# A chunked delta-rule scan: two alternating places for the memory, the query's read moved behind the output product

## What is computed

```python
def step(state, inp):
    w_c, u_c, attn_c, q_c, k_c, e_c = inp
    v_new = u_c - einsum('bhcd,bhde->bhce', w_c, state)
    o_c = einsum('bhcd,bhde->bhce', q_c, state) + einsum('bhcm,bhme->bhce', attn_c, v_new)
    state = state * e_c[..., None, None] + einsum('bhcd,bhce->bhde', k_c, v_new)
    return state, o_c
s0 = zeros((bsz, nh, dk, dv))
_, o = lax.scan(step, s0, ...)
```

## Time and profile before

| | |
|---|---|
| runs, median (range) | 2157.25 us (2155.11 to 2157.98) |
| the profiled execution: span from first to last instruction | 2150.7 us |
| what lies around that span, by the runs | 4.4 to 7.3 us; the profiled execution's own whole time isn't on the page |
| instructions | 20753 |
| PE busy | 2070.0 us |
| DVE busy | 1364.1 us |
| ACT busy | 642.5 us |
| POOL busy | 234.5 us |
| mean granted clock of PE | 0.993 |
| DMA | 207.17 MB, mean 96 GB/s |

### The profile page before, as it was taken

How to read it: one execution, slowest core, us unless ns; L and a number is a source line. 1 busy time by engine, 2 the same in 40 slices (tenths; PEclk the granted TensorE clock), 3 DMA queues, 4 the chain that set the end, 5 groups by cost and what they waited for, 6 DMA issues and landing times. The chain is left out here.

```text
span 2150.7 us, 20753 instructions
## 1 busy us (share of the span) xinstructions
PE 2070.0 (96%) x6898; PEld 1060.6 (49%) x6898; DVE 1364.1 (63%) x1918; ACT 642.5 (30%) x1063; POOL 234.5 (11%) x188
## 2 busy tenths in 40 slices
PE   6999999999999999999899899999999999999998
PEld 5444444446555556566555445554444444444443
DVE  4687753265746746647652578529999997534633
ACT  4345431323443434434311521012321111241021
POOL 0000001112212113122100400001000000003200
PEclk8999999999999999999999999999999999999999
DMA  9333389241111111111420316269722222334021
GB/s 342 110 109 100 116 272 236 89 92 35 47 29 37 38 37 37 24 36 43 147 41 1 108 59 120 74 189 250 173 59 75 68 73 69 103 103 137 20 98 59
DMA packets 243824, 207.17 MB, mean 96 GB/s; under 512 B 52204, under 2 KB 202785, under 8 KB 243745
## 3 DMA queue, kind: packets, MB, share of 16 engines
q1 hardware_dynamic: 213393, 157.25, 24.5%
q0 software_dynamic: 13056, 42.99, 8.2%
q10 hardware_dynamic: 17312, 6.10, 1.2%
HBM read 182.55 MB, written 60.33 MB: 113 GB/s over the span
## 5 line engine op out<-in xcount | busy, mean ns | idle before, releaser
L2300 PE MATMUL bank<-hT,ring 128*128 128x512 f32 x576 | 254.2, 592 | 0.0
L2300 PE MATMUL bank<-resid,ring 128*128 128x512 f32 x432 | 191.3, 592 | 0.0
L2300 PEld LDWEIGHTS bank<-hT,ring 128*128 128x128 f32 x576 | 109.5, 190 | 137.7 <-issue 136.7
L1279 PE MATMUL bank<-hT,ring 128*128 128x512 f32 x336 | 157.7, 595 | 1.8 <-ACT silu_z L1515 1.8
L3220 DVE SCALAR_TENSOR_TENSOR yT<-s_arena,yT 128x1024 f32<-128x1024 f32 x120 | 153.8, 1282 | 0.0
L3220 DVE SCALAR_TENSOR_TENSOR s_arena<-s_arena 128x1024 f32<-128x1024 f32 x112 | 143.5, 1282 | 0.0
L2272 PE MATMUL bank<-hT,ring 128*128 128x512 f32 x320 | 139.4, 594 | 0.0
L2300 PEld LDWEIGHTS bank<-resid,ring 128*128 128x128 f32 x432 | 82.1, 190 | 103.3 <-issue 102.3
L1869 DVE SCALAR_TENSOR_TENSOR memory<-memory,col_exp_last,bank 128x128 f32<-128x128 f32 x64 | 22.3, 348 | 153.7 <-PE bank L1459 153.7
L2272 PEld LDWEIGHTS bank<-hT,ring 128*128 128x128 f32 x320 | 60.2, 190 | 73.7 <-issue 73.4
L2345 PE MATMUL bank<-ssm_y,ring 128*128 128x512 f32 x192 | 83.4, 592 | 0.0
(11 more groups left out here) (585 smaller groups left out, 3671.7 us busy)
## 6 DMA issues: line engine op xcount, KB each, us to landing
ada<-in_ada_w SPq DMA_DIRECT2D x8, 2048.0 KB, 8.1
ring<-in_gdn_in_w SPq DMA_DIRECT2D x32, 512.0 KB, 4.1
ring<-in_w_in SPq DMA_DIRECT2D x54, 256.0 KB, 2.9
ab_U_sums<-in_w_in POOLq DMA_DIRECT2D x6, 2048.0 KB, 19.0
resid<-in_x SPq DMA_DIRECT2D x8, 1024.0 KB, 8.9
ring<-in_lru_in_w SPq DMA_DIRECT2D x16, 512.0 KB, 3.9
ring<-ab_U_sums SPq DMA_DIRECT2D x32, 256.0 KB, 3.0
lru_arena<-in_ada_w SPq DMA_DIRECT2D x6, 1024.0 KB, 12.5
```

The costliest lines, as they stand in the source:

```text
L1279: last = nc.tensor.matmul(bank[:, to, :], w[:, k, :], v[:, k, :], start=(first and k == 0), stop=(k == KB - 1), skip_group_check=not only)
L2300: last = nc.tensor.matmul(bank[:, to, :], w[:, k, :], src[:, k, :], start=(start and k == 0), stop=(k == HK - 1), skip_group_check=not alone)
```

## The change

The memory gets two places that alternate: chunk c reads place c % 2 and its update writes place (c + 1) % 2. The query's read of chunks 1 to 6 moves behind the chunk's output product and gets a mark (`q`); in chunk 7 it stands between the first fill and "new". Chunk 0 has neither read nor query's read nor delta nor output sum: "new" takes the values directly, and DVE copies the memory product into place 1. Chunk 7 has no memory product and no update. The wait for ACT's output step moves from the query's read to "new"; the update gets a wait for the update before it, the output sum one for the query's read. Chunk 0 has one fill fewer in middle heads, and the fills ahead of `k_flip` become 5; in head 7 the counts stay the same in sum (0 and 4 in place of 2 and 2 in chunk 0). The memset goes.

```diff
-            memory = sb("memory", [P, P], scope)
+            memory = sb("memory", [P, 2, P], scope)
...
+            def scan_products(c):
+
+                if c == 0:
+                    return ("new", "mem", "o")
+                return ("read", "new", "mem", "o", "q") if c < NCH - 1 else ("read", "q", "new", "o")
+
+            def scan_sums(c):
+
+                return ("mem",) if c == 0 else ("delta", "mem", "o") if c < NCH - 1 else ("delta", "o")
...
-                        fill(4, 0)
+                        fill(5, 0)
...
-                        for c in range(NCH):
-                            if c == 0:
-                                fill(1, 0)
-                                hd_dve.wait(pe, "invT64b", h)
-                                hd_dve.wait(pe, "mem_zero", h)
-                                hd_dve.wait(pe, "v_tok", h)
-                            else:
-                                hd_dve.wait(pe, f"mem{c - 1}", h)
-                            hd_pe.mark(nc.tensor.matmul(R4[:, 0, :], kT[:, c, :], memory[:, :], start=True, stop=True), f"read{c}")
-                            if c:
+                        def read(c):
+
+                            hd_dve.wait(pe, f"mem{c - 1}", h)
+                            hd_pe.mark(nc.tensor.matmul(R4[:, 0, :], kT[:, c, :], memory[:, c % 2, :], start=True, stop=True), f"read{c}")
+
+                        def query_read(c):
+
+                            if c > 1:
                                 hd_dve.wait(pe, f"o{c - 1}", h)
-                                hd_act.wait(pe, f"o{c - 1}", h)
-
-                            nc.tensor.matmul(R5[:, 4, :], qT[:, c, :], memory[:, :], start=True, stop=True)
+                            hd_pe.mark(nc.tensor.matmul(R5[:, 4, :], qT[:, c, :], memory[:, c % 2, :], start=True, stop=True), f"q{c}")
+
+                        def solve(c, right):
+
+                            hd_pe.mark(nc.tensor.matmul(R4[:, 4, :], invT[:, c, :], right, start=True, stop=True), f"new{c}")
+
+                        def use(c):
+
+                            hd_act.wait(pe, f"new{c}", h)
+                            if c < NCH - 1:
+                                hd_dve.wait(pe, "k_rest", h)
+                                hd_pe.mark(nc.tensor.matmul(R5[:, 0, :], k_rest[:, c, :], delta[:, 1, :], start=True, stop=True), f"mem{c}")
+                            hd_pe.mark(nc.tensor.matmul(R4[:, 4, :], attnT[:, c, :], delta[:, 1, :], start=True, stop=True), f"o{c}")
+
+                        fill(1, 0)
+                        hd_dve.wait(pe, "invT64b", h)
+                        hd_dve.wait(pe, "v_tok", h)
+                        solve(0, v_tok[:, 0, :])
+                        fill(1, 4)
+                        use(0)
+                        for c in range(1, NCH):
+                            read(c)
                             fill(1, 2)
+                            if c == NCH - 1:
+                                query_read(c)
                             hd_dve.wait(pe, f"delta{c}", h)
-                            hd_pe.mark(nc.tensor.matmul(R4[:, 4, :], invT[:, c, :], delta[:, 0, :], start=True, stop=True), f"new{c}")
+                            hd_act.wait(pe, f"o{c - 1}", h)
+                            solve(c, delta[:, 0, :])
                             fill(1, 2)
...
+                            use(c)
+                            if c < NCH - 1:
+                                query_read(c)
...
-                        hd_dve.wait(act, f"o{c}", h)
+                        if c:
+                            hd_dve.wait(act, f"o{c}", h)
+                        else:
+                            hd_act.wait(act, "o0", h)
...
-                        hd_pe.wait(dve, f"o{NCH - 1}", h, back=1)
-                        hd_dve.mark(dve.memset(memory[:, :], 0.0), "mem_zero")
-                        for c in range(NCH):
+                        hd_pe.wait(dve, "mem0", h)
+                        hd_dve.mark(dve.tensor_copy(memory[:, 1, :], R5[:, 0, :]), "mem0")
+                        for c in range(1, NCH):
...
-                            hd_pe.wait(dve, f"mem{c}", h)
-                            hd_dve.mark(dve.scalar_tensor_tensor(out=memory[:, :], in0=memory[:, :], scalar=cols["exp_last"][:, h, c:c + 1],
-                                                                 in1=R5[:, 0, :], op0=ALU.mult, op1=ALU.add), f"mem{c}")
+                            if c < NCH - 1:
+                                hd_pe.wait(dve, f"mem{c}", h)
+                                hd_dve.wait(dve, f"mem{c - 1}", h)
+                                hd_dve.mark(dve.scalar_tensor_tensor(out=memory[:, (c + 1) % 2, :], in0=memory[:, c % 2, :],
+                                                                     scalar=cols["exp_last"][:, h, c:c + 1],
+                                                                     in1=R5[:, 0, :], op0=ALU.mult, op1=ALU.add), f"mem{c}")
                             hd_act.wait(dve, f"o{c}", h)
+                            hd_pe.wait(dve, f"q{c}", h)
```

More of the change, by code:

```diff
@@ L1023, in block_program @@
             o_tok, o_normed = part0[:, :, :], AT
-            memory = sb("memory", [P, P], scope)
+            memory = sb("memory", [P, 2, P], scope)
             delta = sb("delta", [P, 2, P], scope)
             g_rows = delta[0:HEADS * NCH, 0, :]
-            fold_ab = memory[:, 0:2 * HEADS]
+            fold_ab = memory[:, 0, 0:2 * HEADS]
             g_dram = nc.dram_tensor("g_scratch", (HEADS * NCH, P), F32, kind="Internal").ap()
@@ L1038, in halves @@
                 return [n + x for n in names for x in "ab"]
+            def scan_products(c):
[4 more added lines that the diff above has]
+                return ("mem",) if c == 0 else ("delta", "mem", "o") if c < NCH - 1 else ("delta", "o")
             hd_pe = Steps(sem("gdn_pe"), ["k_flip", "kk", "q_flip", "qk"]
                           + [n for s in levels for n in halves(f"Y{s}") + (["v_flip"] if s == levels[0] else []) + halves(f"YT{s}") + (halves(f"F{s}") if s < 64 else [])]
-                          + [f"{n}{c}" for c in range(NCH) for n in ("read", "new", "mem", "o")] + ["o_flip"])
+                          + [f"{n}{c}" for c in range(NCH) for n in scan_products(c)] + ["o_flip"])
             hd_act = Steps(sem("gdn_act"), ["k_sq", "decay", "q_silu", "q_sq", "k_rms", "v_silu"]
@@ L1053, in block_program @@
                            + [n for s in levels for n in halves(f"invT{s}") + (["q_inv", "q_dec"] if s == levels[1] else [])]
-                           + ["mem_zero"] + [f"{n}{c}" for c in range(NCH) for n in ("delta", "mem", "o")]
+                           + [f"{n}{c}" for c in range(NCH) for n in scan_sums(c)]
                            + ["o_inv", "o_tok", "y"])
```

## The result

The changed kernel takes 2119.49 us (median of 4 runs, 2117.52 to 2120.40), against 2157.48 us (4 runs) of the kernel before on the same chip: ratio 0.983, 95% interval 0.9815 to 0.9846, 38.0 us less. The forecast was 2115.8. The profiled execution took 2120.4 us, its span 2118.5.

A forecast was written before the change was run, and what follows sets the result against it. PE, 96% busy, idles 0.97 us per 3.79 us chunk, mostly at the query's read waiting for DVE's output sum. Seven middle scans 35.5 plus last head 6.0 make 41.5 us: 2157.25 - 41.5 = 2115.8 us, range 2109 to 2127.

The forecast's parts named there:

- Steady chunks: Chunks 1 to 6 of a middle scan: 3.30 us from read to read in place of 3.79, 0.49 less each.
- First and last chunk: Middle scan: first chunk 1.52 us shorter, with the copy taken as 0.29; last chunk 0.61 shorter.
- The moved fill: Fifth fill ahead of the key flip, seven times: fits PE's hole to 0.1 us; cost 0, bound 6.0 us.
- Last head: Last head's scan: 1.26 us less in the first chunk, 0.68 in six, 0.69 in the last; 6.0 in sum.
- From the barrier on: Next stage behind the last head: a barrier opens it and its loads are issued relative to it; no change priced.
- The span: Profiled span of the whole kernel: 2150.7 less 41.5, so 2109.2 us.
- 1 (met waits free, 3.18): Added met waits cost nothing: 0.61 us less per steady chunk, 46.5 in sum, time 2110.8; chance 0.20.
- 2 (gain handed back at the seams): Moved fill costs 6.0 us, or query's read doesn't fit behind output product, 9.2: 2121.8 or 2125.0; chance 0.12.
- 3 (copy locked out by POOL): First chunk's new DVE copy held by POOL sums, up to 1.27 us in seven heads, 8.9: 2124.7; chance 0.04.
- Rival 4 (lockstep): Output sum waits for the query's read and delays the next delta: all 48 chunks pay 0.3, 2171.6; chance 0.02.
- 5: Another chain (ring loads, clock) holds the head, scan's gain becomes a wait: 2157, chance 0.02; half lost, 2136, 0.04.
- the rule quoted in the prediction: At the new copy: copies and tensor-scalars can enter a two-port mode locking out GpSimd and themselves for the whole instruction.

The follow-up runs named there:

- d: Kernel before with two memory places and the moved query's read, ends and fills as before, no update wait for the update before it: 2126.36 us, 0.9862.
- g: Changed kernel with a third, always-met wait at the update, behind the other two: 2122.78 us, 0.9845.
- h: Changed kernel with the moved fill put back into chunk 0 (four ahead of the key flip, two behind the first "new"): 2122.97 us, 0.9844.
- a: Changed kernel measured again without edit: 2120.66 us, 0.9832.
- j: Changed kernel measured a third time without edit: 2119.61 us, 0.9833 against the kernel before at 2155.76.
- b: Kernel before, unedited, a single execution again: 2157.16 us, span 2155.2.
- f: Changed kernel with the met waits written ahead of the one that counts, at the update, "new" and the output sum: 2112.41 us, 0.9791.
- k: Changed kernel with met waits ahead of the counting ones and the update's wait for the update before it left out: 2111.94 us, 0.9794.
- c: Kernel before with two alternating memory places alone, nothing moved: 2155.52 us, 0.9995.
- e: Changed kernel with the query's read put back between read and fill in chunks 1 to 7: 2143.67 us, 0.9949.

## Why the prediction was right, and what it missed

The sign, the mechanism and the parts held; the median came out 3.7 us above the forecast, inside the range (2109 to 2127). Against the kernel before on the same chip the gain was 38.0, 36.4 and 36.2 us, 3.5 to 5.3 short of the 41.5. Step by step:

- *Steady chunks.* Forecast 3.30 us, measured 3.30. Right, also in the split: 0.61 from the moved read (d has 3.22), 0.08 given back at the update (d against the changed kernel) and 0.03 to 0.05 at "new". The price, 0.08 for a met wait behind the one that counts, came from one row of another engine, and g doubled it on DVE. In the last head the same query's read, with the same two waits, loads 0.06 behind the sum (1146.37 + 0.35 to the 1146.78 of the earlier trace rows), so no price is paid there; the last section has why.
- *First and last chunk.* The copy measured 0.29, as taken between its bounds, and the read stands at 517.32 (forecast 517.38); from the last read to the last output product it is 2.49, as worked out. Scan 24.42, forecast 24.4.
- *The moved fill.* Forecast: the flip slips by up to 0.1, priced at 0. It slips 0.09 at each flip of heads 1 to 6. With the scan's 5.02 in place of 5.07 this is the missing 1.0 us of 41.5: 7 x 0.14. h shows the other side: without the move each head is 0.86 longer. In head 0 the slip is taken up too, but not where the prediction had it: the key flip is 0.92 later, the query flip, whose wait of 0.46 us is gone, 0.30 later, and the value flip comes at 499.66 for 499.73, with a wait of 0.72 for 0.80 (0.83 and 0.82 in a and j).
- *Last head.* Forecast 6.0 less, measured 6.06; reads 4.81 apart. The start of its scan was to move from 1140.25 to 1104.8 and is at 1105.77.
- *From the barrier on.* This is the step that failed: "behind the last head a barrier opens the next stage, whose loads are issued relative to it", so the next block's time was taken as unchanged. It is 1.9 us longer, by the granted clock of its first 47 us. 1.0 and 1.9 make 2.9 of the 3.7 us. The rest isn't placed. In the traces the first "new" of head 0 stands anywhere from 512.5 to 519.2 us, with no order by version, and the three pairs of medians differ among themselves by 1.8 us.
- *The span.* 2109.2 was forecast and 2118.5 measured, 9.3 more: 1.0 and 1.9 as above, and 6.4 at the loads of yT, since the profile of before was of an execution in which they came early (6.2 of it came back in b). The same kernel again had a span of 2155.2. The prediction saw that the runs lay above that profile by 4.4 to 7.3 us and used the median for the time. What lies around the span is 1.9 or 2.0 us in every run since, so that execution took some 2152.6 us, less than any of the three runs beside it; it could have asked which stretch of the profile was the short one.

The rivals: 1 (met waits free, 3.18) was wrong for the kernel as changed and is right for the same waits in another order (f). 2 (gain handed back at the seams) is refuted by the flip at 548.48 without idle time, by 0.44 from memory product to query's read, and by h. 3 (copy locked out by POOL): all eight copies take 291 or 292 ns, and six of them run wholly within a POOL sum, such as the copy of head 0 (516.97 to 517.26):

```profile
L1888 DVE COPY memory<-bank x8: 291/291/292, 517.0 to 1110.0; 128x128 f32<-128x128 f32 x8
516.55 1.27 POOL L1227 TENSOR_TENSOR yT<-ring 128x512 f32<-128x512 f32 x1 [10.43 <-DMA ring<-in_gdn_in_w]
```

None of the six is stretched (in h no POOL operation falls on a copy, and they take 291 to 293 ns), so this POOL operation doesn't lock the copy out. The Trainium skill, VectorE: DVE Perf Modes, Mode 2×_2P, says that mode doesn't exist for an operand in PSUM, as DVE has one read port there. The trace agrees; it is the reading that the rule quoted in the prediction lacked. Rival 4 (lockstep): delta still waits for PE by 0.17, so the sum is never late. 5: the scan's gain arrives at the barrier, but for the 0.09 us at each seam.

## What to carry to other kernels

Price each link of a loop that PE and another engine hand back and forth, one by one, and look for work that stands in such a link although its result is wanted only later; here one 0.22 us product cost 0.61. In a loop whose index is in a register, write waits that are long met ahead of the wait that decides: here the order alone was worth 5.5 to 6 us of 2120 by the traces (the medians fell by 7 to 8). In straight-line code with constants the decisive one belongs first. And compare a stretch that a change shouldn't touch with a second profile of the same kernel before a difference there is explained.

## What was not expected of the hardware

- Order of waits. In the heads whose index is in a loop register a met wait costs 0.08 to 0.09 us behind the deciding one (memory product to update 0.52, 0.60, 0.69 us with none, one, two of them) and nothing ahead of it (f and k both 3.18). The traces show what fills the time: register operations of 40 ns on the queue, about 0.09 apart. One at the update's own line stands ahead of each update of the middle heads, in every version; in the changed kernel these are 42 of the 48.

```profile
L1902 DVEq ALU_OP  x42: 40/40/40, 520.1 to 1011.7; - x42
```

  For each further wait that is written behind the deciding one, one more stands at the line of `wait` (L58). In g there are two, ahead of the update of 520.80:

```profile
L58 DVEq ALU_OP  x2: 40/40/40, 520.5 to 520.6; - x2
```

  The handover goes by their number: 0.42 us with none (the copy in all heads, and the updates of the last head where no separate wait stands ahead of them, as below), 0.51 to 0.52 with one (d, f, k), 0.60 with two, 0.69 with three. In k the one that is left starts 0.09 ahead of the update that waited, so it stands behind the wait and not under it. A kernel that works these values out ahead of the wait wasn't tried.
- In the last head, whose numbers are constants, there are no register operations and the order is reversed: met wait ahead 0.49 to 0.50 us from memory product to update (1126.79 to 1127.29 in f), behind it or absent 0.42 (1114.34 to 1114.76 in the changed kernel). PE's query's read reverses too: behind the end of the output sum it loads after 0.12 us in the middle heads and 0.05 in the last with the met wait behind (c), and after 0.05 and 0.12 with it ahead (e). The trace of f has a separate wait instruction right ahead of that update:

```profile
L58 DVEq EVENT_SEMAPHORE  x1: 21/21/21, 1127.2 to 1127.2; - x1
```

  It starts 0.43 behind the memory product, about when a lone wait's update starts, and the update follows 0.07 later. By the semaphores in the trace it waits for PE, that is, it is the wait that was written last. In the changed kernel the separate one is again the wait written last, there the long met one: it stands ahead of the memory product and costs nothing. The Trainium skill, Perfetto Trace Analysis, Identifying Dependency Chains, says that an instruction which waits on several engines may get separate wait instructions ahead of it. The trace agrees for the last head (21 ns each here); which wait becomes the separate one the page doesn't say.
- The granted clock behind a barrier: the same instructions, with the last 20 us ahead at the full clock, fall to 1.2 GHz once, twice or three times within 32 us, according to the version (first part 45.6 to 47.5 us), and the two versions that were traced more than once repeat their own pattern (g, whose scans are 0.09 a chunk longer, shares that of the changed kernel). What sets it stays open.
- The wait for scattered loads of yT in the next block: 0.30 us in the first trace of the kernel before, 4.83 in the second, and 2.65 to 5.51 in the other eleven, although the loads are issued at the same distance from the block's first part in all of them.
